# A first block's output gate: group norms moved by a panel and a pair, and merged tiles split one by one

## The reference, cut to what matters

```python
y = y_diag + y_off + x32 * d_skip...                       # state-space branch, 1024 channels
y = y * jax.nn.silu(z)                                     # z = part of hn @ w_in
yg = y.reshape(bsz, seq, 4, 256)
yg = yg * lax.rsqrt(jnp.mean(yg * yg, axis=-1, keepdims=True) + EPS)
yc = yg.reshape(...) * norm_g
gates = jax.nn.sigmoid(g_raw + b_gate)                     # g_raw = part of hn @ w_in
merged = (gates[:, :, 0] * (ya @ w_branch_a) + gates[:, :, 1] * (yb @ w_branch_b)
          + gates[:, :, 2] * (yc @ w_branch_c))
h = h + merged @ w_out
```

## Time and profile before

| what | us |
|---|---|
| median of 3 runs (lowest, highest) | 3615.69 (3615.03, 3619.08) |
| the profiled execution, its own time | 3612.49 |
| its span (first to last instruction) | 3610.7 |
| PE busy in the span | 3450.0 (96%) |
| DVE busy | 1965.9 (54%) |
| ACT busy | 1360.0 (38%) |
| POOL busy | 214.2 (6%) |

### The profile page before, as it was taken

One profiled execution on the slowest core, in us unless ns is written; L12 is line 12 of the kernel. 1 busy time (PEld: TensorE's weight loads), 2 busy tenths in 40 slices (PEclk: granted clock), 3 DMA queues, 4 the chain that ended last, 5 costly groups with the idle time before them and its releaser, 6 DMA issues.

```text
span 3610.7 us, 42003 instructions
## 1 busy us (share of the span) xinstructions
PE 3450.0 (96%) x15516; PEld 2783.8 (77%) x15516; DVE 1965.9 (54%) x2680; ACT 1360.0 (38%) x1914; POOL 214.2 (6%) x158
## 2 busy tenths in 40 slices
PE   7999799899999999999898999999999999989999
PEld 6777667678888888876775888888888777768887
DVE  3677755545445655568653534464445984444444
ACT  3454333423223333345543323242323564343223
POOL 1000000000000000017200000000000550000000
PEclk9999989999999999999999999999999999999999
DMA  4333212223223333332121233333333221213332
GB/s 134 82 93 94 71 36 59 70 88 113 93 94 103 96 93 93 88 94 81 60 82 47 82 102 96 91 96 105 93 90 91 82 75 63 85 47 94 103 95 82
DMA packets 425594, 310.27 MB, mean 86 GB/s; under 512 B 17256, under 2 KB 423200, under 8 KB 425440
## 3 DMA queue, kind: packets, MB, share of 16 engines
q1 hardware_dynamic: 422880, 302.13, 28.1%
q0 software_dynamic: 1664, 4.52, 0.4%
q10 hardware_dynamic: 896, 1.54, 0.1%
HBM read 306.06 MB, written 2.10 MB: 85 GB/s over the span
## 4 chain that ended last, share of the span: by engine, by line
PE 87%; DVE 8%; ACT 3%; issue 2%; DMA 0%; ACTq 0%; DVEq 0%; POOL 0%
PE G L674 77%; PE G L800 2%; DVE w_lo L1818 1%; DVE arena L1671 1%; PE G L663 1%; PE B L663 1%; ACT w_hi L1122 1%; DVE small L1670 1%; PE G L619 1%; PE B L540 1%; PE B L581 1%; DVE y_lo L1833 1%; PE B L522 1%; PE B L873 0%; PE B L771 0%
## 5 line engine op out<-in xcount | busy, mean ns | idle before, releaser
L1122 ACT ACTIVATE w_hi<-raw 128x1024 fp32r<-128x1024 f32 x580 | 615.1, 1061 | 1594.4 <-PE G L674 1569.6
L674 PE MATMUL G<-xn_hi,w_hi 128*128 128x512 f32 x2864 | 1139.7, 398 | 16.6 <-DVE w_lo L1818 16.5
L1818 DVE TENSOR_TENSOR w_lo<-raw,w_hi 128x1024 fp32r<-128x1024 f32 x580 | 720.9, 1243 | 774.2 <-ACT w_hi L1122 771.8
L674 PE MATMUL G<-xn_lo,w_hi 128*128 128x512 f32 x2864 | 1118.4, 390 | 0.0
L674 PE MATMUL G<-xn_hi,w_lo 128*128 128x512 f32 x2864 | 1118.2, 390 | 0.0
L674 PEld LDWEIGHTS G<-xn_hi,w_hi 128*128 128x128 f32 x2864 | 540.1, 189 | 148.9 <-issue 33.6
L674 PEld LDWEIGHTS G<-xn_lo,w_hi 128*128 128x128 f32 x2864 | 540.1, 189 | 120.1 <-issue 9.8
L674 PEld LDWEIGHTS G<-xn_hi,w_lo 128*128 128x128 f32 x2864 | 539.6, 188 | 113.2
L674 PE MATMUL G<-y_hi,w_hi 128*128 128x512 f32 x1472 | 578.3, 393 | 8.6 <-DVE y_lo L1833 8.6
L674 PE MATMUL G<-y_lo,w_hi 128*128 128x512 f32 x1472 | 575.5, 391 | 0.0
L674 PE MATMUL G<-y_hi,w_lo 128*128 128x512 f32 x1472 | 575.3, 391 | 0.0
(11 more groups left out here) (353 smaller groups left out, 2829.5 us busy)
## 6 DMA issues: line engine op xcount, KB each, us to landing
raw<-in_w_in SPq DMA_DIRECT2D x128, 512.0 KB, 4.6
raw<-in_ffn_w_gate SPq DMA_DIRECT2D x88, 512.0 KB, 4.0
raw<-in_ffn_w_up SPq DMA_DIRECT2D x88, 512.0 KB, 5.2
raw<-in_ffn_w_down SPq DMA_DIRECT2D x64, 512.0 KB, 4.0
raw<-in_w_mlp_up SPq DMA_DIRECT2D x32, 512.0 KB, 4.6
raw<-in_w_mlp_down SPq DMA_DIRECT2D x32, 512.0 KB, 4.2
raw<-in_xa_wkv SPq DMA_DIRECT2D x32, 512.0 KB, 4.4
raw<-in_w_out SPq DMA_DIRECT2D x24, 512.0 KB, 4.3
```

Of the source, the lines that this page charges most:

```text
L674: m = pe.matmul(bank[:, 0:n], a[:, k, kt, :], b[:, kt * S:kt * S + n], start=(kt == 0 and t == 0), stop=(kt == nk - 1 and t == 2))
L1122: act.activation(w_hi[:, k], raw[:, 1 - q, :, k * P:(k + 1) * P], ACT.Copy).then_inc(s_whi, 1)
L1818: dve.tensor_tensor(w_lo[:, k], raw[:, 1 - q, :, k * P:(k + 1) * P], w_hi[:, k].bitcast(F32), ALU.subtract)\
```

## The change

It has two parts, both in the first block.

**The norms.** On PE `group_sums(i-1)` stands behind panel (i,1) and not behind (i,0); `group_sums(3)` behind cgate's panel (0,1). On ACT the squares of group i stand at the end of pair i itself, the root of group i-1 ahead of them, and the high parts of group i-2 behind the first Silu of pair i. DVE follows: the low parts and the normalizing of group i-2 stand in the first half of pair i, mean and reciprocal of group i-1 at its end.

**The buffers.** In the whole first mixer the normed input lives in `y_hi`/`y_lo` (now also called `n_hi`, `n_lo`), and the branch outputs in `xn_hi`/`xn_lo` (`b_hi`, `b_lo`). cmix thus reads `xn`, and `y` is free when cgate ends. The merged tile of each cmix panel is split as soon as it is summed: on ACT behind the panel's `prep`, on DVE behind the panel's `prep_lo`, which itself now stands behind the product and the sum.

```diff
+        n_hi, n_lo, b_hi, b_lo = y_hi, y_lo, xn_hi, xn_lo
...
+            normed, branch = (n_hi, n_lo), (b_hi, b_lo)
...
-            gemm("z", xn, unroll=True, after=lambda i, k: group_sums(i - 1) if i and k == 0 else None)
-            gemm("cgate", xn, unroll=True, after=lambda i, k: group_sums(3) if (i, k) == (0, 0) else None)
-            gemm("cmix", y, unroll=True, ready=by_tile(z_v, ("lo",)))
+            gemm("z", normed, unroll=True, after=lambda i, k: group_sums(i - 1) if i and k else None)
+            gemm("cgate", normed, unroll=True, after=lambda i, k: group_sums(3) if (i, k) == (0, 1) else None)
+            gemm("cmix", branch, unroll=True, ready=by_tile(z_v, ("lo",)))
             gemm("wo", y, ready=by_tile(split_v, ("merged",)))
...
             for i in range(NPAIR["z"]):
...
                     prep(n, q, LANDED[n + 1], k)
-                    if i and k == 0:
-                        group_squares(i - 1)
                     product(n, k)
...
-                    if i and k == 0:
-                        group_root(i - 1)
+                    if i >= 2 and k == 0:
+                        group_norm(i - 2)
                 if i:
-                    group_norm(i - 1)
+                    group_root(i - 1)
+                group_squares(i)
...
-                    if (i, k) == (0, 0):
-                        group_squares(3)
-                    if (i, k) == (0, 1):
-                        group_root(3)
-                    if (i, k) == (1, 0):
-                        group_norm(3)
...
+                    if (i, k) == (0, 0):
+                        group_norm(2)
+                    if (i, k) == (0, 1):
+                        group_root(3)
+                    if (i, k) == (1, 0):
+                        group_norm(3)
+
+            def merged_hi(i, k, n):
+
+                if k == 0:
+                    act.wait_ge(split_v.sem, split_v.at("sum", 2 * i))
+                else:
+                    act.wait_ge(s_free, n + 1)
+                j = 2 * i + k
                 act.activation(cut(y_hi, j), cut(merged, j), ACT.Copy).then_inc(split_a.sem, split_a.mark("merged", j))
+
+            only_prep("cmix", merged_hi)
...
                 for k in range(2):
                     prep_lo(n, q, k)
-                    if i and k == 0:
-                        group_rstd(i - 1)
-                for k in range(2):
                     if k == 0:
                         dve.wait_ge(z_a.sem, z_a.at("silu", 2 * i))
...
+                    if i >= 2 and k == 0:
+                        group_norm(i - 2)
                 if i:
-                    group_norm(i - 1)
+                    group_rstd(i - 1)
...
             for i in range(NPAIR["cmix"]):
...
-                    prep_lo(n, q, k)
...
                     ins = dve.tensor_tensor(cut(merged, j), cut(merged, j), cut(c_gate, j), ALU.add)
                     if k == 1:
                         ins.then_inc(s_free, 1)
-            for j in range(KT):
-                dve.wait_ge(split_a.sem, split_a.at("merged", j))
-                lo_of(cut(y_lo, j), cut(merged, j), cut(y_hi, j)).then_inc(split_v.sem, split_v.mark("merged", j))
+                    else:
+                        ins.then_inc(split_v.sem, split_v.mark("sum", j))
+                    prep_lo(n, q, k)
+                    dve.wait_ge(split_a.sem, split_a.at("merged", j))
+                    lo_of(cut(y_lo, j), cut(merged, j), cut(y_hi, j)).then_inc(split_v.sem, split_v.mark("merged", j))
```

More of the change, by code:

```diff
@@ L736, in turn_x @@
                 turn(("x", j), [x_in[:, t, j * P:(j + 1) * P] for t in range(NB)], (turn_v, ("x", j)))
-            gemm("v", xn, unroll=True, ready=by_tile(norm_v, ("lo", 0)), after=turn_x)
+            gemm("v", normed, unroll=True, ready=by_tile(norm_v, ("lo", 0)), after=turn_x)
             def gmlp_turns(i, k):
@@ L749, in gmlp_turns @@
                         turn(("v", j), [vt[:, j * S + t * P:j * S + (t + 1) * P] for t in range(NB)], (gmlp_a, ("v", j)))
-            gemm("u", xn, unroll=True, after=gmlp_turns)
+            gemm("u", normed, unroll=True, after=gmlp_turns)
             def mix():
@@ L775, in _ @@
                 n = P0[f"{name}{i}"]
-                pair(f"{name}{i}", i, n, n % 2, xn, xn if name == "lru" else y, S,
+                pair(f"{name}{i}", i, n, n % 2, normed, normed if name == "lru" else branch, S,
                      by_tile(gmlp_v, ("lo",), 1) if (name, i) == ("ga", 0) else None)
@@ L783, in _ @@
                     lru_gates(i + 1)
-            gemm("xbc", xn, unroll=True)
-            gemm("dt", xn)
+            gemm("xbc", normed, unroll=True)
+            gemm("dt", normed)
             def half_kv(l, x):
@@ L815, in panel_of_gb @@
                 pe.wait_ge(s_wlo, 2 * n + k + 1)
-                panel(k, G[k], *(y if k else xn), KTS["gb"], S).then_inc(s_mm, 1)
+                panel(k, G[k], *(branch if k else normed), KTS["gb"], S).then_inc(s_mm, 1)
             pe.wait_ge(s_free, P0["dt"])
@@ L1256, in _ @@
                 act.wait_ge(full.sem, full.at("xs", j))
-                act.activation(cut(xn_hi, j), B[BANK.get(("xs", j), 0)][:, :], ACT.Copy, scale=col("norm_mix_g", j))\
+                act.activation(cut(n_hi, j), B[BANK.get(("xs", j), 0)][:, :], ACT.Copy, scale=col("norm_mix_g", j))\
                    .then_inc(norm_a.sem, norm_a.mark("hi", 0, j))
@@ L1326, in lru_hi @@
                 act.wait_ge(s_mm, 2 * P0["ga7"] + 2)
-                act.activation(cut(y_hi, j), cut(lru_y, j), ACT.Copy).then_inc(lru_a.sem, lru_a.mark("hi", j))
+                act.activation(cut(b_hi, j), cut(lru_y, j), ACT.Copy).then_inc(lru_a.sem, lru_a.mark("hi", j))
             for name, i in SLOTS:
@@ L1336, in _ @@
                         act.wait_ge(gmlp_v.sem, gmlp_v.at("y", g))
-                        act.activation(cut(y_hi, g), tmp(4 + g % 2), ACT.Copy).then_inc(gmlp_a.sem, gmlp_a.mark("hi", g))
+                        act.activation(cut(b_hi, g), tmp(4 + g % 2), ACT.Copy).then_inc(gmlp_a.sem, gmlp_a.mark("hi", g))
                     act.activation(small[:, 16:24], par[:, COL["lru_lambda"]:COL["lru_lambda"] + 8], ACT.Abs)\
@@ L1385, in group_squares @@
                 for k in range(2):
-                    act.wait_ge(z_v.sem, z_v.at("gated", 2 * g + k))
+                    if k == 0:
+                        act.wait_ge(z_v.sem, z_v.at("gated", 2 * g + 1))
                     if g >= 1:
@@ L1397, in group_norm @@
                     act.wait_ge(z_v.sem, z_v.at("y", 2 * g + k))
-                    act.activation(cut(y_hi, 2 * g + k), tmp(4 + k), ACT.Copy).then_inc(z_a.sem, z_a.mark("hi", 2 * g + k))
+                    act.activation(cut(b_hi, 2 * g + k), tmp(4 + k), ACT.Copy).then_inc(z_a.sem, z_a.mark("hi", 2 * g + k))
             for i in range(NPAIR["z"]):
@@ L2107, in mixed @@
                         dve.wait_ge(gmlp_a.sem, gmlp_a.at("hi", g - 1))
-                        lo_of(cut(y_lo, g - 1), tmp(4 + (g - 1) % 2), cut(y_hi, g - 1))\
+                        lo_of(cut(b_lo, g - 1), tmp(4 + (g - 1) % 2), cut(b_hi, g - 1))\
                             .then_inc(gmlp_v.sem, gmlp_v.mark("lo", g - 1))
@@ L2156, in lru_lo @@
                 dve.wait_ge(lru_a.sem, lru_a.at("hi", j))
-                lo_of(cut(y_lo, j), cut(lru_y, j), cut(y_hi, j)).then_inc(lru_v.sem, lru_v.mark("lo", j))
+                lo_of(cut(b_lo, j), cut(lru_y, j), cut(b_hi, j)).then_inc(lru_v.sem, lru_v.mark("lo", j))
             for name, i in SLOTS:
@@ L2232, in group_norm @@
                     dve.wait_ge(z_a.sem, z_a.at("hi", j))
-                    lo_of(cut(y_lo, j), tmp(4 + k), cut(y_hi, j)).then_inc(z_v.sem, z_v.mark("lo", j))
+                    lo_of(cut(b_lo, j), tmp(4 + k), cut(b_hi, j)).then_inc(z_v.sem, z_v.mark("lo", j))
             for i in range(NPAIR["z"]):
```

8 lines of the change are left out of this document (3 added, 5 removed).

## The result

| | before | after |
|---|---|---|
| median of the runs beside each other, us | 3617.39 (4 runs) | 3594.82 (4 runs) |
| lowest and highest, us | 3615.03, 3619.42 | 3590.70, 3600.17 |
| profiled execution: own time, span, us | 3612.49, 3610.7 | 3600.17, 3598.4 |
| end of z(0,0) to end of wo(0,0), us | 159.54 | 137.62 |

The ratio after to before is 0.9941, 95% interval 0.9928 to 0.9953, so the change makes the kernel 0.6% faster, 22.6 us by the medians. A second series of the changed kernel gave 0.9944 (0.9931 to 0.9958). By the medians that series has 17.4 us (3598.24 against 3615.61). In the stretch that the change touches 21.92 us are gone; forecast were 21.8.

The account below looks back on a forecast made before the run. PE was taken as the bound (busy 96% of the span), losing time to waits and low clock; 24 x 5.44 + 4 x 1.80 = 137.8 us in the stretch, 21.8 less, gave 3593.9 us against the median 3615.7, range 3588 to 3602.

Parts of the forecast that it names:

- The sum: From z(0,0) to wo(0,0): 24 panels at 5.44 us plus four sums at 1.80, 137.8 us, so 21.8 less.
- The price of a sum that PE doesn't wait for: Group sums on PE: 1.80 us each, twice the next phase's 0.90 for a half-long sum; from a standstill 2.08.
- The causes: The stretch's 21.8 us by cause: 15.3 of PE waits, about 5.2 of low clock, 1.3 of slower restarts.
- Slack, first half: Pairs in z: second `prep` queued behind ACT's high parts, 0.4 us late; its `w_lo` has 4.5 us slack.
- Slack, second half: Pairs in z: `w_lo` behind the reciprocal ends at 15.1, PE wants it at 18.1; slack 3.0 us, smallest in z.
- E0: End of panel (i,0) in z, the zero of the slack count; the next panel ends at E0 + 5.4 us.
- cmix: Last merged tile ready 3.4 us behind the last panel, wanted by wo at 4.8: slack 1.4, the 5.2 us wait goes.
- Table loads: ACT in z: 1.28 us by the rows; the skill's about 2.7 would cut the smallest slack to about 1.2.
- The rival of the clock that doesn't come back: In the stretch, low-clock pieces only move, so 5.2 us of gain are missing: 3599.1 us; chance 0.08.
- late tail: z pairs' second half over 3.0 us longer, `w_lo` holds PE each pair, gain only 11.9 us: 3603.8; chance 0.07.
- no gain: Behind wo another engine sets the pace and the time is lost again: 3615.7 us; chance 0.04.
- slower: ACT's high parts ahead of the second `prep` wait for DVE, PE stalls in z and cgate: 3623 us; chance 0.03.

Follow-up runs that it names:

- recip_1: Changed kernel with each of the four group-norm reciprocals computed twice, 3.35 us more on DVE each; stretch 142.67 us, whole 3605.93 us, ratio 0.9969 to before.
- The two parts by themselves: Changed kernel cut to moved norms: stretch 145.91 us, ratio 0.9960; cut to exchanged buffers with merged tiles split one by one: 152.15 us, 0.9984 (ratios to before).
- the filled waits: Kernel before with useless matmuls in PE's waits (7 ahead of each sum, 9 in cgate, 21 ahead of wo); stretch 154.10, again 154.09; ratios 0.9998, 0.9993.
- late_tile: Changed kernel with one useless 3.35 us reciprocal on DVE ahead of the last merged tile's low part; stretch 140.30 us, whole 3599.16 us, ratio 0.9957 to before.
- variants without fill: Against before: norms moved alone, 3601.13 us; buffers exchanged and merged tiles split one by one, 3607.85; buffers exchanged alone, 3616.06; before 3614.87.
- slowed kernels: Changed kernel with useless reciprocals on DVE: each group-norm one computed twice, 3605.93 us, or three times, 3613.70; one ahead of the last merged tile's low part, 3599.16.
- padded: Changed kernel with 12 or 24 useless matmuls ahead of wo; stretch 140.34 and 143.07 us, whole 3601.55 and 3602.98 us, ratios 0.9960 and 0.9963 to before.
- split_only: Changed kernel with the norms back in their old order, keeping exchanged buffers and merged tiles split one by one; stretch 152.15 us, whole 3607.85, ratio 0.9984 to before.

## Why the prediction was right

**The sum.** Forecast were 21.8 us less in the stretch, 137.8; it is 21.92 less, 137.62. The whole was forecast at 3593.9 and measured at 3594.8, inside the range of 3588 to 3602. For the profiled execution the prediction gave 3590.7, and it took 3600.17. The sum left everything outside the stretch as it was, and this profile spent 9.6 us more there than that of before. So the size of the gain in the stretch is the mechanism's; that the median of the whole came within 1 us is in part luck.

**The price of a sum that PE doesn't wait for**, taken from a sum half as long at 1.80, was (137.62 - 24 x 5.44) / 4 = 1.77 us. The row of the next phase was the right one to lean on, and the price from a standstill, 2.08, the wrong one.

**The causes.** Waits 15.3, low clock 5.2, restarts 1.3; the last is a remainder and wasn't measured by itself. The prediction called 625.03 a start from a standstill, but that row has no idle time before it. The price it took from there, 5.85 us for such a panel, holds all the same: in `recip_1`, from real standstills at full clock, 689.79 and 703.28, the next marks come after 5.79 and 5.82 us. The waits are gone row by row. The two parts by themselves gave 13.6 and 7.4 of forecast 14.4 and 7.5. That the low clock follows the waits was argued; the filled waits show it in the stretch: 5.44 us back without anything being ready earlier, against the 5.2 counted for the clock.

**Slack, first half.** The second `prep` was forecast 0.4 us late and is 0.2 late.

**Slack, second half.** Here is a mistake in the count. The prediction put PE's wish for the next `w_lo` at E0+18.1, but a second sum stands on PE before that panel, so it is 19.9, and the slack in one pair is 4.8 us and not 3.0. It changed nothing in the sum. One pair's slack also isn't the slack of the row of pairs: one added reciprocal of 3.35 us should cost nothing by it, yet cost 5.05 us over four pairs, since a late reciprocal delays the next pair's normalizing, with it ACT's `prep`, and so the next reciprocal. The order by hand over all pairs, in the expectation of that run, gave 5.1.

**cmix.** The slack of tile 7 was forecast as 1.4; the trace shows 1.5, and the late tile shows 1.5 by its wait.

**Table loads.** The row of 1.28 us held after the change too (656.59 in ACT's timeline). The 2.7 us of the Trainium skill's "ScalarE: Activation LUTs", section "Step-by-step: what each stage is for", isn't seen as time on ACT here.

**The rival of the clock that doesn't come back** was given 8 in 100 and 5.2 us. In the stretch it is wrong. For the whole it is partly right, in another form: the profiled executions of the changed kernel lose 6 us more to the low clock in the second block's attention than those of before, and so do those of the filled kernel, whose whole gained little. The changed kernel's median of 3594.8 hides that its times lie in two groups, near 3591.5 and 3599; in the second series the median fell into the upper group, at 3598.2. That the kernel is about 0.6% faster came twice (0.9941 and 0.9944). To have the whole to 1 us was luck at that place.

**What stays open**: what decides whether the clock falls behind those waits of the attention. It isn't the length of the wait, nor the chip: the three later series ran on three chips, and each has profiles of both kinds. Why the eight profiles of before, of its variants without fill, and of the slowed kernels were at the short end, and the six of the changed, padded and filled kernels at the long end, isn't settled. That the two groups of whole times are the short and the long attention fits in size (6 us, and up to 2.7 in the late piece), and the profiles of `recip_1` and `late_tile` are short and belong to their lower groups; but each kernel has one or two profiles, so it is argued. The other rivals (late tail, no gain, slower) have no trace.

## What to carry to other kernels

Where an engine's queue holds "convert weights when the panel ends" next to helper work, put the helper work one step later than its input is ready and one step ahead of its use; here two such moves took all waits from 138 us. Price such a move by marks that the bound engine sets in another engine's timeline: the distance with nothing between, the distance with one item, times their counts. And count slack over the whole row of repeats, not in one: a delay that one pair hides comes back in the next.

## What the runs showed of the hardware that was not expected

- The same wait of 2.1 us, at the same instruction, with the same program around it, was followed by a granted clock of 1.00 over 8 us in eight profiles and of 0.79 in six.
- In the stretch, of four waits of 1.8 to 2.0 us one was followed by the low clock: the third in before, the fourth in `split_only`. The waits of 1.82 and 2.37 us in `recip_1` were not; the one of 1.87 us in `late_tile` was.
- Useless matmuls in a wait keep the clock up: 58 of them (four times 7, 9 and 21) gave 5.4 us back in the stretch.
- Times of one kernel can lie in two groups 7 us (0.2%) apart: 3590.7, 3591.7, 3591.7, 3592.2 and 3597.5, 3598.2, 3599.2, 3599.7, 3600.2. A median over four or five such runs moves by several us with one run.
